# Order of the expert units in a two-layer hybrid decoder trunk: light units in groups of eight, two of them behind the last gate piece, five early loads as single units

## The chip, the cores and the metric

The kernel runs on one core of one Trainium2 chip. The metric is device time in microseconds (us) of one execution; lower is better. The profile is one execution recorded by the hardware profiler.

## The reference

The program is a causal trunk of two layers over 256 tokens with 1024 channels, float32. Each layer adds a mixer (differential attention and retention, gated and projected) and then a feed-forward block: a dense SwiGLU block in layer 0, and in layer 1 a mixture of eight experts of which each token uses two.

```python
def swiglu(x, w1, w3, w2):
    return (jax.nn.silu(x @ w1) * (x @ w3)) @ w2

def moe(hn, w_router, w1, w3, w2):
    ...
    top_v, top_i = lax.top_k(logits, TOP_K)
    top_w = jax.nn.softmax(top_v, axis=-1)
    ...
    for e in range(N_EXPERTS):
        out = out + combine[:, e:e + 1].astype(t.dtype) * swiglu(t, w1[e], w3[e], w2[e])
```

The change touches only the expert block: 1024 to 2816 to 1024, eight times.

## The kernel before

**Units.** Weights come from HBM in units of 128 partitions by 2048 float32, 1 MiB each. An expert has 33 units: 22 hold w1 and w3 (numbers 0 to 21), 11 hold w2 (22 to 32). Eight experts are 264 units, 264 MiB. They are loaded in pairs of two units (2 MiB, one DMA), the last unit of an expert alone. `LOADS` is the list of these 136 loads in the order of issue, all from the SP queue. They go round a ring of six buffers of two units (`RING = 6`), so load i may be issued only when what load i-6 brought is no longer needed.

**Two kinds of unit.** The experts are worked in the order of their token counts; p is the place in it. For p in `CHAIN` (0, 1, 3, 5) up to 128 rows are held, and a weight unit is used in split form: ScalarE copies it to `wh` (L616), VectorE takes the rest to `wl` (L634), and TensorE makes three products for each of four chunks, 12 matmuls (L639 to L641). There are three slots of `wh` and `wl`, and a unit is split two units of this kind ahead (`AHEAD = 2`), so the split of one waits until TensorE has used the one three before it. I call these split units. For p in `SMALL` (2, 4, 6, 7) at most 64 rows are held; TensorE multiplies the loaded unit as it is, in two halves of 64 columns of the array (`few_halves`, L1737). I call these light units, and write 5.30 for unit 30 of place 5.

**When a buffer comes free.** In `load_ring`, a load that follows a split load waits for `lo_ready` of its last unit (both units split), one that follows a light load waits for `unit_used` (TensorE has multiplied both).

**The order.** `moe_orders` walks the split loads and puts two light loads (four units) in front of a split load whenever that many are due. `TAKEN`, unit by unit `IN_USE`, is the order in which all compute engines work; there the light loads stand one split load earlier than in `LOADS`. Both begin and end alike: 0.0 to 0.7, 0.22, 0.23 first, and 5.30, 5.31, 5.32 followed by the light units 7.18 to 7.32 last. Before, TensorE works 31 groups of light units, nearly all of four.

**Gate pieces.** w1 and w3 are worked in slices of 512 columns (the last of 256). After each slice TensorE's result goes through ScalarE (sigmoid, L1147), VectorE (L2413, L2420), four or, for the last, two transposes on TensorE (`g_transposes`, L1263), ScalarE (L1155) and VectorE (L2426), and only then may the units of w2 that use it be multiplied. In `large_unit` of TensorE the transposes of the last piece stand behind unit 30, and units 31 and 32 wait for `g_lo`. The text calls this the last turning; that of place 5 is the last of the program.

**The end.** After 5.32 ScalarE copies the sums to `ys`, GpSimd stores them to HBM and gathers every token's rows back (L844), VectorE adds them (L2441). Beside this TensorE works 7.18 to 7.32 and sums the last expert's rows, which VectorE adds at the very end (L2505), and the result is stored.

Of the kernel before, what the change touches and what calls it, by code (L numbers as in the profile page):

```python
# [52 lines left out]
UNIT = 2048  # L53
RAW, SPLIT = 6, 3
SLICES = FF // 256
IN_GROUPS = IN_W // 512
MIX_UNITS = 2 * IN_GROUPS + 4 + 4
FFN_UNITS = 2 * SLICES + FC // 2
WIDE = FF // 512
# [9 lines left out]
SMALL = (2, 4, 6, 7)  # L69
# [4 lines left out]

CHAIN = tuple(p for p in range(E) if p not in SMALL)
FEW_FROM, FEW_ALONE = 6, 12
RING = 6


def by_slices():  # L80
# [14 lines left out]
def loads_of(p):  # L95

    order = range(FFN_UNITS) if p in SMALL else BY_SLICES
    return [(p, j, min(2, FFN_UNITS - j)) for j in order if j % 2 == 0]


def moe_orders():

    chain = [load for p in CHAIN for load in loads_of(p)]
    few = [load for p in SMALL for load in loads_of(p)]
    n_chain, n_few = (sum(count for _, _, count in loads) for loads in (chain, few))
    loaded, taken, done, n = [], [], 0, 0
    for load in chain:
        loaded.append(load)
        taken.append(load)
        n += load[2]  # L110
        due = max(0, n - FEW_FROM) * (n_few - FEW_ALONE) // (n_chain - FEW_FROM)
        while due - done >= few[0][2] + few[1][2]:
            for _ in range(2):
                loaded.append(few[0])
                taken.insert(len(taken) - 1, few[0])
                done += few.pop(0)[2]
    return loaded + few, taken + few


def units_in(loads):  # L120
    return [(p, j + a) for p, j, count in loads for a in range(count)]


LOADS, TAKEN = moe_orders()
LOADED, IN_USE = units_in(LOADS), units_in(TAKEN)
NUMBER = {unit: MOE_BASE + k for k, unit in enumerate(LOADED)}
USED = {NUMBER[unit]: MOE_BASE + k + 1 for k, unit in enumerate(IN_USE)}
LOAD_OF = {NUMBER[p, j + a]: (i, a) for i, (p, j, count) in enumerate(LOADS) for a in range(count)}


def is_whole(n):

    return MOE_BASE <= n < OVER_BASE and LOADED[n - MOE_BASE][0] in SMALL


def used(n):

    return USED.get(n, n + 1)


SPLITS = [n for n in range(OVER_BASE) if not is_whole(n)]
SPLIT_NO = {n: k for k, n in enumerate(SPLITS)}
# [57 lines left out]
def build(nc, x, boot_d, positions, units_d, pairs_d, lasts_d, zeros_d, cols_d, rows_d, out):  # L200
    ctx = ExitStack()
    with ctx:
# [3 lines left out]
        def sem(name):  # L206
            return ctx.enter_context(nc.semaphore(name))
# [73 lines left out]
        def row(name):  # L281
# [56 lines left out]
        ring = [raw[:, 0:2, :].rearrange("p a n -> p (a n)"), ring_1[:, :], raw[:, 2:4, :].rearrange("p a n -> p (a n)"),  # L338
                raw[:, 4:6, :].rearrange("p a n -> p (a n)"), ring_4[:, :], ring_5[:, :]]
# [10 lines left out]
        landed = [sem(f"landed{s}") for s in range(RAW)]  # L350
        loaded = [sem(f"loaded{s}") for s in range(RING)]
        hi_ready = sem("hi_ready")
        lo_ready = sem("lo_ready")
# [147 lines left out]
        class Units:  # L501
# [40 lines left out]
            def raw(self, j):  # L542

                n = self.number(j)
                if self.in_ring(j):
                    i, half = LOAD_OF[n]
                    return ring[i % RING][:, half * UNIT:(half + 1) * UNIT]
                return raw[:, n % self.raw_slots, :]

            def landed(self, j):  # L550

                n = self.number(j)
                if self.in_ring(j):
                    i, _ = LOAD_OF[n]
                    return loaded[i % RING], 16 * (i // RING + 1)
                s = n % self.raw_slots
                if self.raw_slots == RAW:
                    c = n // RAW + 1
                else:
                    c = len([m for m in range(MOE_BASE) if m % RAW == s])  # L560
                    c += len([m for m in range(OVER_BASE, n + 1) if m % SPLIT == s])
                return landed[s], self.at(16 * c - (16 if s < FIRST else 0), 16 * (self.per // self.raw_slots))
# [10 lines left out]
        def last_in(slots):  # L573

            return max(n for n in range(MOE_BASE) if n % RAW in slots)

        def load_ring(eng, i, e):

            p, j, count = LOADS[i]
            if i >= RING:  # L580
                q, first, n = LOADS[i - RING]
                m = NUMBER[q, first + n - 1]
                eng.wait_ge(*((unit_used, used(m)) if is_whole(m) else (lo_ready, SPLIT_NO[m] + 1)))
            elif i == 1:
                eng.wait_ge(mt_tr, 4 * DEPTH)
            elif i == 4:
                eng.wait_ge(unit_used, MOE_BASE)
            elif i == 5:
                eng.wait_ge(hg_ready, 2)
            else:  # L590
                slots = {0: (0, 1), 2: (2, 3), 3: (4, 5)}[i]
                eng.wait_ge(lo_ready, SPLIT_NO[last_in(slots)] + 1)
            to = ring[i % RING]
            if count == 2:
                eng.dma_start(to, pairs_d[e * (FFN_UNITS // 2) + j // 2]).then_inc(loaded[i % RING], 16)
            else:
                eng.dma_start(to[:, 0:UNIT], lasts_d[e]).then_inc(loaded[i % RING], 16)
# [110 lines left out]
        def _(sp):  # L708
# [28 lines left out]
            for i, (p, _, _) in enumerate(LOADS):  # L737
                if p not in e_of:
                    if len(e_of) == 1:
                        sp.wait_ge(order_ready, 1)  # L740
                    e_of[p] = sp.value_load(otab[0:1, 1 + BY_COUNT[p]:2 + BY_COUNT[p]], min_val=1, max_val=MIDDLE)
                load_ring(sp, i, e_of[p])
# [1933 lines left out]
```

## Time and profile before

| | us |
|---|---|
| median of 3 runs | 1207.55 (1206.71 to 1207.64) |
| the profiled execution, its own time | 1206.29 |
| its span in the profile | 1204.6 |
| TensorE busy | 1189.1 (99%) |
| VectorE busy, ScalarE busy | 741.1 and 593.6 |
| DMA, whole span | 384.82 MB, mean 319 GB/s |

The profiled execution took 1.7 us more than its span, and lies 1.26 us below the median. A busy TensorE in the profile says that matmuls were under way, not that it ran at its peak. The expert block's first load is issued at 509.48 us, its first unit is multiplied at 550.01 us, and the span ends at 1204.6 us.

### The profile page before, as it was taken

What the parts mean: (1) busy time and instruction counts of PE and PEld (TensorE: products, weight loads), DVE (VectorE), ACT (ScalarE), POOL (GpSimd) and SP (SyncE); (2) the same over time, 40 slices, a digit from 0 to 9 for tenths busy, and PEclk for the clock granted to TensorE, in tenths of its full rate; (3) what the DMA queues carried; (4) which work ended last, traced back from release to release, by engine and by line L of the source; (5) the groups of instructions that cost most, each with busy time, mean ns of one, the idle gap of its engine ahead of it and who ended that gap; (6) DMA issues with size and microseconds to landing.
All of it is one profiled execution on the core that took longest, in us unless ns stands there. A gap on an engine that the chain in (4) does not pass through costs nothing.

```text
span 1204.6 us, 15901 instructions
## 1 busy us (share of the span) xinstructions
PE 1189.1 (99%) x6454; PEld 916.8 (76%) x6454; DVE 741.1 (62%) x765; ACT 593.6 (49%) x641; POOL 68.0 (6%) x55
## 2 busy tenths in 40 slices
PE   9999999999999999999999999999999999999997
PEld 8878888888888888888777766777667777577764
DVE  6867765656545857767757565665646665564633
ACT  7667445434336467445554454453535444453420
POOL 0600001000000600000000000000000000000001
PEclk9999999999999999999999999999999999999999
DMA  9753557655555453378999999999999999999997
GB/s 378 310 185 130 177 177 286 217 176 178 205 180 186 159 208 113 111 277 340 384 427 425 427 426 427 427 429 427 426 427 428 427 427 428 426 428 428 427 425 292
DMA packets 36590, 384.82 MB, mean 319 GB/s; under 512 B 4337, under 2 KB 4337, under 8 KB 7985
## 3 DMA queue, kind: packets, MB, share of 16 engines
q1 hardware_dynamic: 34672, 374.83, 77.2%
q0 software_dynamic: 1696, 8.66, 2.0%
q8 instruction: 53, 0.87, 0.3%
q10 hardware_dynamic: 144, 0.26, 0.1%
q14 instruction: 25, 0.20, 0.0%
HBM read 379.80 MB, written 7.61 MB: 322 GB/s over the span
## 4 chain that ended last, share of the span: by engine, by line
PE 86%; DMA 6%; issue 3%; DVE 3%; POOL 1%; ACT 1%; SPq 0%; POOLq 0%; DVEq 0%; ACTq 0%
PE ps L639 21%; PE ps L641 21%; PE ps L640 21%; PE ps L1737 16%; DMA raw<-in_pairs 4%; PE ps L1263 3%; DVE wl L634 1%; DMA h<-in_x 1%; DMA back<-y_rows,yidx 1%; PE ps L1625 1%; POOL rst L777 1%; PE ps L1637 1%; PE ps L1322 1%; ACT wh L616 0%; DVE h L2441 0%
## 5 line engine op out<-in xcount | busy, mean ns | idle before, releaser
L634 DVE TENSOR_TENSOR wl<-raw,wh 128x2048 fp32r<-128x2048 f32 x152 | 350.5, 2309 | 200.0 <-ACT wh L616 199.6
L616 ACT ACTIVATE wh<-raw 128x2048 fp32r<-128x2048 f32 x152 | 291.1, 1918 | 211.1 <-PE ps L641 167.5
L639 PE MATMUL ps<-wh,XT 128*128 128x512 f32 x856 | 340.1, 397 | 0.3 <-DVE wl L634 0.3
L641 PE MATMUL ps<-wh,XT 128*128 128x512 f32 x856 | 333.9, 390 | 0.0
L640 PE MATMUL ps<-wl,XT 128*128 128x512 f32 x856 | 333.4, 389 | 0.0
L634 DVE TENSOR_TENSOR wl<-ring,wh 128x2048 fp32r<-128x2048 f32 x66 | 151.0, 2291 | 89.8 <-ACT wh L616 89.2
L639 PEld LDWEIGHTS ps<-wh,XT 128*128 128x128 f32 x856 | 160.7, 188 | 40.3 <-issue 8.1
L641 PEld LDWEIGHTS ps<-wh,XT 128*128 128x128 f32 x856 | 160.6, 188 | 34.3
L640 PEld LDWEIGHTS ps<-wl,XT 128*128 128x128 f32 x856 | 160.9, 188 | 31.5
L616 ACT ACTIVATE wh<-ring 128x2048 fp32r<-128x2048 f32 x66 | 126.4, 1915 | 95.4 <-PE ps L641 70.1
L1737 PE MATMUL ps<-ring,few_X 128*64 128x256 f32 x704 | 80.6, 381 | 1.5 <-DMA ring<-in_pairs 1.5
L1737 PE MATMUL ps<-raw,few_X 128*64 128x256 f32 x704 | 80.4, 381 | 1.0 <-DMA raw<-in_pairs 1.0
L639 PE MATMUL ps<-wh,moe_gT_h 128*128 128x512 f32 x176 | 70.9, 403 | 2.1 <-DVE moe_gT_l L2426 2.1
L1737 PEld LDWEIGHTS ps<-ring,few_X 128*64 128x64 f32 x704 | 50.4, 137 | 28.1 <-issue 6.5
L1737 PEld LDWEIGHTS ps<-raw,few_X 128*64 128x64 f32 x704 | 49.5, 137 | 28.3 <-issue 5.8
L640 PE MATMUL ps<-wl,moe_gT_h 128*128 128x512 f32 x176 | 69.4, 394 | 0.0
L641 PE MATMUL ps<-wh,moe_gT_l 128*128 128x512 f32 x176 | 69.2, 393 | 0.0
L1737 PE MATMUL ps<-raw,few_gT 128*64 128x256 f32 (+1 forms) x272 | 44.2, 470 | 0.0
L639 PEld LDWEIGHTS ps<-wh,moe_gT_h 128*128 128x128 f32 x176 | 33.4, 190 | 12.9 <-issue 3.9
L942 ACT ACTIVATE mix<-ps,rn 128x512 f32<-128x512 f32 x40 | 26.0, 687 | 27.2 <-PE ps L641 27.1
L641 PEld LDWEIGHTS ps<-wh,moe_gT_l 128*128 128x128 f32 x176 | 33.5, 190 | 7.3
L640 PEld LDWEIGHTS ps<-wl,moe_gT_h 128*128 128x128 f32 x176 | 33.4, 190 | 6.5
(294 smaller groups left out, 1149.1 us busy)
## 6 DMA issues: line engine op xcount, KB each, us to landing
raw<-in_pairs SPq DMA_DIRECT2D x65, 2048.0 KB, 17.6
ring<-in_pairs SPq DMA_DIRECT2D x63, 2048.0 KB, 17.6
raw<-in_units SPq DMA_DIRECT2D x86, 1024.0 KB, 5.0
ring<-in_lasts SPq DMA_DIRECT2D x4, 1024.0 KB, 15.6
raw<-in_lasts SPq DMA_DIRECT2D x4, 1024.0 KB, 17.2
y_rows<-in_zeros POOLq DMA_DIRECT2D x7, 512.0 KB, 7.9
raw<-in_boot SPq DMA_DIRECT2D x5, 512.0 KB, 7.6
y_rows<-ys POOLq DMA_DIRECT2D x4, 512.0 KB, 10.6
```

The costliest lines, as they stand in the source:

```text
L616: nc.scalar.activation(wh[:, U.split_slot(j), :], U.raw(j), ACT.Copy).then_inc(hi_ready, 1)
L634: nc.vector.tensor_tensor(wl[:, s, :], U.raw(j), wh[:, s, :].bitcast(F32), ALU.subtract).then_inc(lo_ready, 1)
L639: nc.tensor.matmul(o, xh, bh, start=start, stop=False)
L640: nc.tensor.matmul(o, xh, bl, start=False, stop=False)
L641: return nc.tensor.matmul(o, xl, bh, start=False, stop=stop)
L777: nc.gpsimd.tensor_tensor(to, of, nhalf[:, 0:of.shape[-1]], ALU.pow).then_inc(rs_ready, 1)
L942: ins = nc.scalar.activation(to, acc, ACT.Copy if g < 6 else ACT.Sigmoid, scale=rn[:, t:t + 1])
L1263: return nc.tensor.transpose(o, i, ident)
L1322: last = nc.tensor.matmul(ps[:, (6, 6, 4)[k] + c, a * n:(a + 1) * n], qkT[part, hd, tok[t]], qkT[part, 4 + hd, 0:n], start=True, stop=True)
L1625: last = nc.tensor.matmul(ps[:, ROWS_AT[n], a * P:(a + 1) * P], xs[:, at:at + P], sel[:, t * SEQ:t * SEQ + P], start=t == 0 and a == 0, st ...
L1637: last = nc.tensor.matmul(ps[:, FEW_ROWS[n], a * P:(a + 1) * P], xs[:, at:at + P], sel[:, t * SEQ + P:(t + 1) * SEQ], start=t == 0 and a == 0,
L1737: last = nc.tensor.matmul(o[at], x, of[half], start=start, stop=stop, tile_position=(0, half * FEW))
```

## The change

`GROUPED = 4`: light loads are taken four at a time, eight units. The order becomes, for example, 0.0 to 0.7, 0.22, 0.23, 0.8 to 0.11 (fourteen split units), 2.0 to 2.7, then eight split units, eight light ones and so on; 17 groups in place of 31. `with_turning_covered` takes the two light units that stand last in front of 5.30 and puts them behind it, in the order of work alone. `SINGLY` is loads 7 to 11: each becomes two DMAs of one unit, and each of those waits only for the split of the unit that lay in its half of the buffer; the counts of landed loads are changed to fit.

```diff
+GROUPED = 4
 RING = 6
+SINGLY = range(RING + 1, 2 * RING)
...
-        while due - done >= few[0][2] + few[1][2]:
-            for _ in range(2):
+        while due - done >= sum(count for _, _, count in few[:GROUPED]):
+            for _ in range(GROUPED):
...
+def with_turning_covered(units):
+
+    first = (CHAIN[-1], 2 * SLICES + 2 * WIDE - 2)
+    few = [unit for unit in units[:units.index(first)] if unit[0] in SMALL][-2:]
+    rest = [unit for unit in units if unit not in few]
+    at = rest.index(first) + 1
+    return rest[:at] + few + rest[at:]
...
-LOADED, IN_USE = units_in(LOADS), units_in(TAKEN)
+LOADED, IN_USE = units_in(LOADS), with_turning_covered(units_in(TAKEN))
...
+            if i in SINGLY:
+                q, first, _ = LOADS[i - RING]
+                for a in range(2):
+                    eng.wait_ge(lo_ready, SPLIT_NO[NUMBER[q, first + a]] + 1)
+                    at = slice(a * UNIT, (a + 1) * UNIT)
+                    eng.dma_start(ring[i % RING][:, at], pairs_d[e * (FFN_UNITS // 2) + j // 2][:, at])\
+                        .then_inc(loaded[i % RING], 16)
+                return
```

How it moves instructions is seen at three places. The first is the SP queue from load 5 on (in the first fence, from the sixth load of the ring; buffers 0, 2 and 3 of the ring print as `raw`). Before:

```order
L595 DMA ring<-in_pairs 128x4096
L741 TENSOR_LOAD otab
L741 ISA x2
L595 ISA
L595 DMA raw<-in_pairs 128x4096
L595 ISA
L595 DMA ring_63<-in_pairs 128x4096
L595 DMA raw<-in_pairs 128x4096 x2
```

The same place with the change:

```order
L619 DMA raw<-in_pairs 128x4096
L601 DMA ring_63<-in_pairs 128x2048 x2
L765 TENSOR_LOAD otab
L765 ISA x2
L601 ISA
L601 DMA raw<-in_pairs 128x2048
```

Load 6 no longer brings a light pair but 0.10 and 0.11, so it stands ahead of the read of the experts' order (`otab`), and load 7 (0.24, 0.25) and those behind it are halves of 2048 columns.

The second place is VectorE from the split of 0.22 to the first pieces of place 2 (`wl` is the split, `moe_gbuf` and `moe_gT_l` belong to the gate pieces of split experts, `few_` to light ones). Before:

```order
L634 TENSOR_TENSOR wl<-ring_64,wh 128x2048 x2
L2420 TENSOR_TENSOR moe_gbuf<-ps,moe_gbuf 128x512
L634 TENSOR_TENSOR wl<-ring,wh 128x2048 x2
L2458 TENSOR_TENSOR few_gbuf<-ps,few_sgm 128x256
L2426 TENSOR_TENSOR moe_gT_l<-ps,moe_gT_h 128x512
L634 TENSOR_TENSOR wl<-raw,wh 128x2048 x2
L2413 TENSOR_TENSOR moe_gbuf<-ps,moe_sgm 128x512
L634 TENSOR_TENSOR wl<-raw,wh 128x2048 x2
```

With the change:

```order
L658 TENSOR_TENSOR wl<-ring_64,wh 128x2048 x2
L2444 TENSOR_TENSOR moe_gbuf<-ps,moe_gbuf 128x512
L658 TENSOR_TENSOR wl<-ring,wh 128x2048 x2
L2450 TENSOR_TENSOR moe_gT_l<-ps,moe_gT_h 128x512
L658 TENSOR_TENSOR wl<-raw,wh 128x2048 x2
L2437 TENSOR_TENSOR moe_gbuf<-ps,moe_sgm 128x512
L658 TENSOR_TENSOR wl<-ring_63,wh 128x2048 x2
L2482 TENSOR_TENSOR few_gbuf<-ps,few_sgm 128x256
```

The splits of 0.10, 0.11, 0.24 and 0.25 now stand ahead of the first light group's work.

The third place is TensorE at the last turning, from the last matmuls of 5.30 to the first of 5.31 (`cols,moe_gbuf` are the turning's transposes, L1761 with the change is L1737 before). Before:

```order
L641 MATMUL ps<-wh,moe_gT_l 128x512
L1263 MATMUL ps<-cols,moe_gbuf 128x128 x2
L639 MATMUL ps<-wh,moe_gT_h 128x512
L640 MATMUL ps<-wl,moe_gT_h 128x512
```

With the change:

```order
L665 MATMUL ps<-wh,moe_gT_l 128x512
L1287 MATMUL ps<-cols,moe_gbuf 128x128 x2
L1761 MATMUL ps<-ring,few_X 64x256 x16
L1287 MATMUL ps<-cols,few_gbuf 128x128 x2
L663 MATMUL ps<-wh,moe_gT_h 128x512
L664 MATMUL ps<-wl,moe_gT_h 128x512
```

Two light units, 7.16 and 7.17, and the two transposes of their expert's piece now stand between the turning and 5.31.

## Rows read from the trace of the kernel before

**Rows 1.** Windows of the core: each engine's busy us, TensorE clock, DMA share, GB/s.

```profile
570.00:575.00 5.00, 5.00 (x26) 4.14 (x24) 4.85 (x4) 4.36 (x4) 0.00 (x0) 1.00 0.47 118
585.00:590.00 5.00, 5.00 (x42) 3.29 (x39) 2.73 (x3) 2.67 (x3) 0.00 (x0) 1.00 0.93 377
600.00:1100.00 500.00, 498.96 (x2888) 356.06 (x2888) 299.39 (x267) 238.72 (x202) 5.09 (x9) 1.00 1.01 427
```

**Rows 2.** Waits: engine, line, what it waited for, us in total, times, longest.

```profile
PE ps L1737 <- DMA ring<-in_pairs: 1.5, 3, 0.6
PE ps L1737 <- DMA raw<-in_pairs: 1.0, 1, 1.0
...
PEld ps L1737 <- issue: 41.1, 136, 1.4
```

**Rows 3.** Timeline of the SP queue, loads 10 to 15 of the ring.

```profile
577.95 5.78 SPq L595 DMA_DIRECT2D ring<-in_pairs  x2
585.68 0.34 SPq L595 DMA_DIRECT2D raw<-in_pairs  x1
589.13 0.34 SPq L595 DMA_DIRECT2D ring<-in_pairs  x1
596.57 5.79 SPq L595 DMA_DIRECT2D raw<-in_pairs  x2
```

**Rows 4.** Windows of one us after a load that starts from rest.

```profile
572.00:573.00 1.00, 1.00 (x6) 0.84 (x5) 1.00 (x2) 1.00 (x1) 0.00 (x0) 1.00 0.71 131
573.00:574.00 1.00, 1.00 (x6) 0.81 (x6) 0.85 (x2) 0.64 (x2) 0.00 (x0) 1.00 0.97 180
574.00:575.00 1.00, 1.00 (x6) 0.84 (x5) 1.00 (x1) 1.00 (x1) 0.00 (x0) 1.00 0.57 229
```

**Rows 5.** Timeline of TensorE around the first light group.

```profile
581.97 3.67 PE L1737 MATMUL ps<-raw,few_X 128*64 128x256 f32 x32
...
589.02 0.50 PE L639 MATMUL ps<-wh,XT 128*128 128x512 f32 x1
```

**Rows 6.** Timeline of ScalarE and VectorE: the split of 0.9.

```profile
578.97 1.92 ACT L616 ACTIVATE wh<-ring 128x2048 fp32r<-128x2048 f32 x1 [0.80 <-PE ps L641]
...
580.92 2.29 DVE L634 TENSOR_TENSOR wl<-ring,wh 128x2048 fp32r<-128x2048 f32 x1 [0.35 <-ACT wh L616]
```

**Rows 7.** Timeline of TensorE from 7.16 to 7.18, the last turning between.

```profile
1145.57 3.67 PE L1737 MATMUL ps<-ring,few_X 128*64 128x256 f32 x32 [0.56 <-DMA ring<-in_pairs]
...
1149.37 0.48 PE L639 MATMUL ps<-wh,XT 128*128 128x512 f32 x1
...
1154.93 0.39 PE L639 MATMUL ps<-wh,moe_gT_h 128*128 128x512 f32 x1
...
1157.71 0.44 PE L1263 MATMUL ps<-cols,moe_gbuf 128*128 128x128 f32 x2
1160.24 0.66 PE L639 MATMUL ps<-wh,moe_gT_h 128*128 128x512 f32 x1 [2.10 <-DVE moe_gT_l L2426]
...
1167.50 4.75 PE L1737 MATMUL ps<-raw,few_X 128*64 128x256 f32 x42
```

**Rows 8.** Timeline of ScalarE and VectorE: splits of 5.30 and 5.31, last piece.

```profile
1150.35 1.92 ACT L616 ACTIVATE wh<-raw 128x2048 fp32r<-128x2048 f32 x1 [8.31 <-DMA raw<-in_pairs]
...
1152.30 4.50 DVE L634 TENSOR_TENSOR wl<-raw,wh 128x2048 fp32r<-128x2048 f32 x2 [6.22 <-ACT wh L616]
...
1157.23 0.42 DVE L2420 TENSOR_TENSOR moe_gbuf<-ps,moe_gbuf 128x256 f32<-128x256 f32 x1
```

**Rows 9.** Window of the core over 5.31, columns as in rows 1.

```profile
1160.00:1164.00 4.00, 3.76 (x10) 2.95 (x11) 0.19 (x1) 0.00 (x0) 0.00 (x0) 0.57 1.01 430
```

**Rows 10.** Chain and timeline at the end: gather back, last sums, last additions.

```profile
1181.51 11.89 DMA back<-y_rows,yidx
...
1195.11 2.00 PE L1823 MATMUL ps<-ys,selT 64*128 64x256 f32 x16
...
1197.58 2.73 DVE L2505 SCALAR_TENSOR_TENSOR h<-ps,comb,h 128x512 f32<-128x512 f32 x4 [0.22 <-DVE h L2441]
```

More of the change, by code:

```diff
@@ L121, in units_in @@
     return [(p, j + a) for p, j, count in loads for a in range(count)]
+def with_turning_covered(units):
[4 more added lines that the diff above has]
+    return rest[:at] + few + rest[at:]
 LOADS, TAKEN = moe_orders()
-LOADED, IN_USE = units_in(LOADS), units_in(TAKEN)
+LOADED, IN_USE = units_in(LOADS), with_turning_covered(units_in(TAKEN))
 NUMBER = {unit: MOE_BASE + k for k, unit in enumerate(LOADED)}
 USED = {NUMBER[unit]: MOE_BASE + k + 1 for k, unit in enumerate(IN_USE)}
+assert all(LOADS[i][2] == LOADS[i - RING][2] == 2 and LOADS[i - RING][0] not in SMALL for i in SINGLY)
 LOAD_OF = {NUMBER[p, j + a]: (i, a) for i, (p, j, count) in enumerate(LOADS) for a in range(count)}
@@ L554, in landed @@
                     i, _ = LOAD_OF[n]
-                    return loaded[i % RING], 16 * (i // RING + 1)
+                    return loaded[i % RING], 16 * len(range(i % RING, i + 1, RING)) + 16 * halved_before(i)
                 s = n % self.raw_slots
@@ L575, in last_in, with halved_before @@
             return max(n for n in range(MOE_BASE) if n % RAW in slots)
+        def halved_before(i):
+            return len([k for k in SINGLY if k <= i and k % RING == i % RING])
         def load_ring(eng, i, e):
             p, j, count = LOADS[i]
+            if i in SINGLY:
[6 more added lines that the diff above has]
+                return
             if i >= RING:
```

## Prediction

> **What bounds the kernel now.** I read the windows first. From 600 to 1100 us the DMA engines are full at 427 GB/s while TensorE is busy 498.96 of 500 us at full clock [rows 1], so either could be the bound. The waits decide: from about 1100 us on TensorE waits for loads, 1.5 and 1.0 us in all [rows 2]. One unit is 1,048,576 bytes, 2.46 us at 427 GB/s. TensorE needs 2.78 us for a split unit (5.56 us for two from 1149.37 to 1154.93 [rows 7]) and 1.76 us for a light one (7.05 us for four [rows 5]); one of each plus its share of transposes is some 4.65 us, against 4.91 us for the two loads. So TensorE starts late, with the ring full, and slowly catches up with a DMA stream that never stops. The end is the place of the stream plus what comes behind it: the pair 5.30, 5.31 lands at 1150.35 [rows 8], 5.32 is multiplied by 1167.5 [rows 7], and from there two chains of nearly equal length run to the end: store and gather back (the gather lands at 1193.4), and fifteen light units with the last sums at 1195.1 to 1197.1. VectorE's last additions start at 1197.58 [rows 10]. Both hang on 5.32, so a delay of 5.32 is a delay of the end, and a gain on one of the chains alone is worth under 0.5 us.
>
> What matters is therefore (1) when the stream becomes full, (2) whether it stays so, (3) the 17.15 us from the landing of 5.30 to the end of 5.32.
>
> **Groups of eight.** The same units are loaded and multiplied; 31 groups become 17. Each switch costs TensorE's queue about 0.3 us (41.1 us in 136 gaps in front of light matmuls [rows 2]), so 14 fewer are at most 4.2 us of TensorE's time. I cost it at nothing: the stream hides it, since TensorE ahead of time only waits longer for loads.
>
> **The stream's start.** Loads 12 and 13 now follow split loads, not light ones. Before, they could be issued at 585.68 and 589.13, when 2.1 and 2.3 were multiplied [rows 3]. Now load 12 waits for the split of 0.11 and load 13 for that of 0.25, and these wait for TensorE's use of 0.8 and 0.10, three split units earlier. 0.8 now starts where the first light unit did, at 581.97 [rows 5], and is used at 584.75; ScalarE's start to VectorE's end is 4.24 us in the split of 0.9 (578.97 to 583.21 [rows 6]); with 0.2 us to start and 0.2 to issue, load 12 goes out at 589.4. Likewise 0.10 is used at 590.2, and load 13 goes out at 594.9.
>
> A load that starts from rest moves 131, 180 and 229 KB in its first three us in place of 427 each [rows 4], a loss of 1.7 us. Before: load 10, issued at 577.95, counts from 579.7 and is through at 584.6; load 11 (the second of the first row, 583.40) follows to 589.5; the window to 590 is short by 0.6 us (377 GB/s [rows 1]); so load 12 moves from 590.1 and load 13 from 595.0. With the change load 11 is through by 588, load 12 starts from rest, counts from 591.1, and load 13 moves from 596.0, 1.0 us later than before. Bounds: 0.3 us later if load 12 loses nothing beyond the 1.0 us until its first packets, 2.0 us if load 13 finds a half-empty queue too. I take **+1.3 us**, nearest to the worked case.
>
> **Single units.** Loads 7 to 11 put their first halves out 2 to 3 us earlier, which fills part of the holes such as 570 to 575 us (118 GB/s [rows 1]). I cost it at nothing, gain or loss: the next load (12) cannot go before 589.4, by which time loads 7 to 11 are through with either form, so what is gained is given back as a longer hole in front of load 12. Nobody waits for them earlier: TensorE's next waits are at 1100 us. The five more issues are 0.33 us each on SP, which otherwise sits in waits. Load 6 no longer waits for the experts' order, but it queues behind load 5 anyway. The Trainium skill, Perfetto Trace Analysis, DMA Optimizations, says that splitting DMAs lets some start sooner where the DMA engines are generally idle; by it the stream would be full earlier, and the sum would lose the 1.3 us and more. That is the first rival below.
>
> **Does the stream stay full?** Load 14 waits for 2.1, now used at about 596.6, and is needed at 601; load 21, at the end of the first eight split units, is free at about 632 and needed at 635. These are the thinnest margins. Sixteen units take TensorE some 37.4 us and the stream 39.3, so the margin grows by 1.9 us a turn. Cost nothing; up to 1 us in the range.
>
> **The last turning.** The loads are the same here, so 5.30 lands at 1150.35 + 1.3 = 1151.65. Before, TensorE was busy with 5.20 and 5.21 until 1154.93 [rows 7], 0.3 us after 5.30's split was ready (1152.30 plus half of 4.50 [rows 8]). Now 7.16 and 7.17 no longer stand in front of them, and TensorE is through early: 7.14 and 7.15 land one pair before 7.16 (1145.5 [rows 7], less 4.9, plus 1.3: 1141.9), take 3.5 us, 5.20 and 5.21 take 5.6, so TensorE stands idle from 1151.1 to 1156.0. Then 5.30 (2.75). The transposes wait 0.3 us for VectorE, which finishes the last piece 0.85 us after the splits (1157.65 against 1156.8 [rows 8], now 1158.95), and take 0.45; 7.16 and 7.17 take 3.5 and their transposes 0.4; the turning's own chain over ScalarE and VectorE is done within that. 5.31 starts 7.5 us after 5.30, before 5.3 (1154.93 to 1160.24, of it 2.1 idle [rows 7]): +2.2 us. 5.31 and 5.32 took 7.26 us, since the clock in the window 1160 to 1164 was 0.57 [rows 9]; without an idle stretch before them they take 5.6: -1.7 us. 5.30's earlier start after landing: -0.3 us. Sum **+0.2 us**: two light units of work, which stood where TensorE had slack, replace an idle stretch and its slow clock, and are worth the same.
>
> **The clock.** An idle stretch of 2.1 us was followed by half clock, 3.4 us long by the loss (7.26 against 5.56 is 1.7 us) [rows 7, 9]. The new idle stretch in front of 5.30 is 4.9 us. If TensorE is at 1.2 GHz when it resumes, 5.30 and what follows lose up to 3 us; nothing if the slow stretch falls into the idle time. The 0.3 us wait for VectorE takes part of it. I take **+1.2 us**, below the 1.7 us of the rows. The Trainium skill, TensorE: Matmul & The Clock Gate, Loop structure matters more than you think, names a DMA wait in front of matmuls as the order that lets the array go cold; by it this change moves the cold stretch from 5.31 to 5.30, and the sum would carry the whole 1.7 us.
>
> **Sum.** 1.3 + 0.2 + 1.2 = +2.7 us on the profiled execution: 1209.0. That execution lies 1.26 us below the median; against the median 1207.55 it is **1210.2 us**.
>
> **Rivals.**
> - The early halves count (faster). If the stream is limited by the holes at 555 to 580 us and load 12's wait is shorter than I work out, the hole of 3.6 us at 570 to 575 (427 less 118 GB/s [rows 1]) comes off: 1204.0. It decides if load 12 is issued before about 586. For: the holes are there. Against: the split of 0.11 needs 0.8 used, and that is TensorE's pace. 8%.
> - TensorE is the bound (faster). Then the 14 switches give up to 4.2 us: 1203.4. For: 498.96 of 500 us busy. Against: the waits for DMA at the end [rows 2] and the full stream. 5%.
> - The stream slips less than 1 us and the slow clock falls into the idle stretch (no difference): 1207.55 + 0.3 to 1.0 + 0.2, 1208.0 to 1208.8. Nothing in the profile excludes it. 39%.
> - The stream is starved in the middle (slower): eight split units in a row free buffers at TensorE's and VectorE's pace, and where load 21's margin of 3 us is gone, each of the first groups leaves a hole of 1 to 3 us: 1211 to 1215. Against: the margins above. 6%.
> - The change does not do what it says: the order shows that it does. Not counted.
>
> **How the numbers follow.** My forecast, slower by 1.5 to 4.5 us, has 42%, most of it past 2.4 us. About 0.2% (2.4 us) is what can be told from no change. Slower by more than that: 40% (34 of my 42, and the starved stream's 6). Within 0.2%: 47% (the 39, and 8 of my case). Faster: 13% (the two rivals). The range reaches from 1206.0, which leaves out the two faster rivals, to 1213.2, which holds the bounds of stream and clock (2.0 + 0.2 + 3.0 is 1212.8) and part of the starved case. Likeliest case's own range: 1209.0 to 1212.0.
>
> **What would show it.** Right: windows from 590 us full at 427 GB/s in both, but load 12 issued at 589 to 590 and load 13 at about 595, a hole around 588 to 590; 5.30 landing 1 to 2 us later, TensorE idle 4 to 5 us in front of 5.30, no idle between the turning's transposes and 5.31, a clock below 1 near 1153 to 1160, 5.32 through at 1169 to 1171. Wrong: windows below 420 GB/s after 600 us, or load 12 before 586, or 5.32 through by 1167.5.

## The result and the profile after

The changed kernel takes **1210.51 us** (median of 9 runs, 1209.66 to 1211.87) against 1207.45 us (9 runs, 1206.16 to 1208.41) for the kernel before on the same chip: ratio 1.0023, 95% interval 1.0015 to 1.0032. It is slower by 3.1 us. The profiled execution has a span of 1207.9 us, before 1204.6. One execution of all those below, of warm_before_last_pair, took 1510.16 us at a mean granted clock of 0.79 and is left out of every median.

**Windows**, columns as in [rows 1].

```profile
570.00:575.00 5.00, 5.00 (x25) 4.15 (x24) 4.85 (x4) 4.64 (x4) 0.00 (x0) 1.00 0.68 223
585.00:590.00 5.00, 5.00 (x24) 4.14 (x23) 4.69 (x4) 3.88 (x4) 0.00 (x0) 1.00 0.65 231
590.00:595.00 5.00, 5.00 (x36) 3.50 (x36) 4.21 (x2) 1.88 (x1) 0.00 (x0) 1.00 0.91 352
600.00:1100.00 500.00, 495.47 (x2873) 358.57 (x2871) 299.97 (x267) 240.26 (x202) 5.11 (x9) 1.00 1.01 427
635.00:640.00 5.00, 5.00 (x50) 3.34 (x48) 0.44 (x2) 0.00 (x0) 0.00 (x0) 1.00 1.01 397
670.00:675.00 5.00, 5.00 (x48) 3.08 (x46) 0.74 (x3) 0.64 (x2) 0.00 (x0) 1.00 1.01 377
```

At 570 us the halves fill part of the hole (223 GB/s for 118 [rows 1]); at 585 the hole is deeper (231 for 377) and reaches into the next window. From 600 to 1100 us the DMA engines are on the whole as full as before (427 GB/s), and TensorE is busy 495.47 us of 500 instead of 498.96: the time it saved became idle time, since the stream sets the pace. Two more dents stand at 635 and 670, with 397 and 377 GB/s where the kernel before has 429 and 439.

**The SP queue** around load 12, at loads 20 and 21, and at the end (us, length of the group of issues).

```profile
575.29 8.05 SPq L601 DMA_DIRECT2D ring<-in_pairs  x4
588.79 0.34 SPq L619 DMA_DIRECT2D raw<-in_pairs  x1
594.23 0.34 SPq L619 DMA_DIRECT2D ring<-in_pairs  x1
...
626.23 7.59 SPq L619 DMA_DIRECT2D raw<-in_pairs  x2
...
1146.58 19.56 SPq L619 DMA_DIRECT2D ring<-in_pairs  x2
```

Load 12 goes out at 588.79 and load 13 at 594.23, where 585.68 and 589.13 stood [rows 3]. Load 21, the second of the fourth row, goes out at 633.49. The last row is the one I had not looked for: load 130 goes out at 1146.58, but load 131, the second of the row, only 19 us later, at 1165.8. Before, load 21 went out at 627.02, and loads 130 and 131 were 4.2 us apart:

```profile
623.04 4.31 SPq L595 DMA_DIRECT2D raw<-in_pairs  x2
...
1145.19 4.56 SPq L595 DMA_DIRECT2D ring<-in_pairs  x2
```

**TensorE at the last turning.** Timeline, with the idle time in front and what ended it.

```profile
1156.79 0.76 PE L663 MATMUL ps<-wh,moe_gT_h 128*128 128x512 f32 x1 [4.73 <-DVE wl L658]
...
1161.94 3.67 PE L1761 MATMUL ps<-ring,few_X 128*64 128x256 f32 x32
...
1171.40 4.97 PE L1761 MATMUL ps<-raw,few_X 128*64 128x256 f32 x44
```

TensorE stands idle 4.73 us in front of 5.30 and not at all in front of 5.31 (2.10 us before [rows 7]). 5.32 is through at 1171.40, 3.9 us later than before. Windows over the same place and behind it:

```profile
1150.00:1155.00 5.00, 2.06 (x10) 1.37 (x8) 0.65 (x1) 2.59 (x2) 0.00 (x0) 0.93 1.00 424
1155.00:1160.00 5.00, 3.21 (x8) 2.56 (x9) 4.90 (x5) 3.19 (x3) 0.00 (x0) 0.50 1.02 436
1160.00:1165.00 5.00, 5.00 (x36) 3.44 (x36) 2.66 (x3) 0.38 (x1) 0.00 (x0) 0.89 0.85 360
1165.00:1170.00 5.00, 5.00 (x27) 3.85 (x24) 0.00 (x0) 0.60 (x1) 0.00 (x0) 1.00 0.83 315
```

The granted clock (third number from the right) is 0.50, the 1.2 GHz level, over 1155 to 1160, and by the three means below 1 for some 6.8 us in all, against 3.4 us before. Some 2.5 of the 6.8 us fall into the idle stretch itself. From 5.30's start to that of the transposes it is 4.84 us (1156.79 to 1161.63), and 2.98 us at full clock (1156.64 to 1159.62 in warm_before_last_pair below), so the slow clock cost TensorE 1.9 us. And the weight stream falls to 360 and 315 GB/s at 1160 to 1170: that is load 131, which came late.

**The end**, as in [rows 10].

```profile
1184.55 9.96 DMA back<-y_rows,yidx
```

```profile
1194.53 2.68 DVE L2465 SCALAR_TENSOR_TENSOR h<-back,tw,h 128x1024 f32<-128x1024 f32 x2 [12.33 <-DMA back<-y_rows,yidx]
...
1198.90 2.00 PE L1847 MATMUL ps<-ys,selT 64*128 64x256 f32 x16
...
1200.02 2.73 DVE L2529 SCALAR_TENSOR_TENSOR h<-ps,comb,h 128x512 f32<-128x512 f32 x4 [0.22 <-DVE h L2465]
```

The gather is four DMAs, issued 1.2 to 1.4 us apart. The row of the changed kernel is the first of them and that of rows 10 the second, so the two can't be set side by side. Before, the first and the additions of the second are

```profile
1180.16 1.05 POOL L844 DMA_INDIRECT back<-y_rows,yidx  x1 [10.74 <-DMA y_rows<-ys]
...
1193.43 1.29 DVE L2441 SCALAR_TENSOR_TENSOR h<-back,tw,h 128x1024 f32<-128x1024 f32 x1 [1.31 <-DMA back<-y_rows,yidx]
```

So the first is issued 4.4 us later than before and is there 9.96 us after its issue, against 10.67 us before (its additions started at 1190.83). The last sums start 3.8 us later, the last additions 2.4 us.

### The profile page after: what moved, and what is told of

Same layout as the page of the kernel before. It is cut to its first block, busy times and chain, and to the rows that moved or that the text cites. A ratio compares the mean times of both kernels' runs of the same rounds, so it can differ in the third digit from the quotient of the medians.

```text
span 1207.9 us, 15914 instructions
## 1 busy us (share of the span) xinstructions
PE 1186.0 (98%) x6454; PEld 919.8 (76%) x6454; DVE 740.6 (61%) x765; ACT 594.2 (49%) x641; POOL 68.0 (6%) x55
## 4 chain that ended last, share of the span: by engine, by line
PE 78%; DMA 13%; DVE 4%; ACT 2%; issue 2%; POOL 1%; SPq 0%; DVEq 0%; POOLq 0%; ACTq 0%
PE ps L663 20%; PE ps L665 20%; PE ps L664 20%; DMA raw<-in_pairs 12%; PE ps L1761 10%; PE ps L1287 3%; DVE wl L658 2%; ACT wh L640 2%; PE ps L1649 1%; DMA back<-y_rows,yidx 1%; POOL rst L801 1%; PE ps L1661 1%; PE ps L1346 1%; PE ps L685 0%; PE ps L689 0%
## 5 line engine op out<-in xcount | busy, mean ns | idle before, releaser
L1761 PE MATMUL ps<-raw,few_X 128*64 128x256 f32 x768 | 87.2, 381 | 3.9 <-DMA raw<-in_pairs 3.9
L1761 PEld LDWEIGHTS ps<-raw,few_X 128*64 128x64 f32 x768 | 56.0, 137 | 32.0 <-issue 8.5
L1761 PE MATMUL ps<-ring,few_X 128*64 128x256 f32 x640 | 73.2, 381 | 1.9 <-DMA ring<-in_pairs 1.9
L1761 PEld LDWEIGHTS ps<-ring,few_X 128*64 128x64 f32 x640 | 46.5, 137 | 24.4 <-issue 4.9
L1189 ACT ACTIVATE few_sgm<-ps 128x256 f32<-128x256 f32 (+1 forms) x24 | 8.7, 361 | 102.7 <-PE ps L1761 102.7
L2482 DVE TENSOR_TENSOR few_gbuf<-ps,few_sgm 128x256 f32<-128x256 f32 (+1 forms) x24 | 9.6, 400 | 67.0 <-ACT few_sgm L1189 58.0
L1761 PE MATMUL ps<-ring,few_gT 128*64 128x256 f32 (+1 forms) x256 | 41.4, 475 | 0.0
```

The lines of the kernel that those rows point to most:

```text
L1761: last = nc.tensor.matmul(o[at], x, of[half], start=start, stop=stop, tile_position=(0, half * FEW))
```

## The experiments

All were timed in five rounds beside the kernel before, whose median was 1207.6 to 1207.7 us (27 to 35 runs); each has 11 runs, first_group_four 4, and the changed kernel the 9 of above. "Shift" is how much later a load's first packet moves than in the kernel before, from the bytes of the packets of the SP queue summed in order. A profiled execution as a whole starts the expert block 0.4 us early to 1.6 us late, so shifts are given less that of load 5, which no edit touches. Read them to 0.1 or 0.2 us. The last column is the profile's own time, without that correction, when the light units behind 5.32 begin (before: 1167.50 [rows 7]).

| kernel | median us | ratio, 95% | shift of load 14 | 30 | 130 | 131 | 5.32 through |
|---|---|---|---|---|---|---|---|
| changed | 1210.51 | 1.0023 (1.0015 to 1.0032) | 1.5 | 2.0 | 2.0 | 3.5 | 1171.40 |
| groups_only | 1209.82 | 1.0017 (1.0008 to 1.0026) | 1.6 | 2.3 | 2.3 | 2.3 | 1169.63 |
| no_singles | 1210.27 | 1.0024 (1.0015 to 1.0033) | 1.6 | 1.7 | 1.6 | 3.2 | 1172.08 |
| no_turning | 1209.61 | 1.0015 (1.0006 to 1.0024) | 1.4 | 2.2 | 2.1 | 2.1 | 1169.74 |
| first_two_fours | 1209.73 | 1.0017 (1.0008 to 1.0026) | -1.9 | 2.3 | 2.3 | 3.1 | 1170.74 |
| singles_only | 1207.78 | 0.9999 (0.9991 to 1.0008) | -2.0 | -0.4 | 0.3 | 0.3 | 1166.33 |
| turning_only | 1208.61 | 1.0007 (0.9998 to 1.0016) | -0.2 | -0.3 | 0.2 | 1.5 | 1169.73 |
| warm_before_last_pair | 1209.68 | 1.0018 (1.0009 to 1.0027) | 1.3 | 1.5 | 1.5 | 2.4 | 1169.43 |
| before_warm_turning | 1207.35 | 0.9998 (0.9989 to 1.0007) | 0.1 | -0.1 | 0.2 | 0.2 | 1166.14 |
| turning_loads_too | 1207.63 | 1.0000 (0.9990 to 1.0009) | -0.1 | -0.3 | -0.1 | -0.1 | 1164.37 |
| change_loads_too | 1209.98 | 1.0021 (1.0012 to 1.0030) | 1.5 | 1.6 | 1.7 | 1.7 | 1166.68 |
| before_late_last_pair | 1208.62 | 1.0006 (0.9997 to 1.0015) | 0.1 | -0.2 | 0.3 | 0.3 | 1170.60 |
| first_group_four | 1223.38 | 1.0136 (1.0121 to 1.0152) | -2.3 | 2.0 | 16.4 | 16.6 | 1164.87 |

### One part, and all but one

```diff
 groups_only:  GROUPED = 4; SINGLY = range(0); IN_USE = units_in(TAKEN)
 no_singles:   SINGLY = range(0)
 no_turning:   IN_USE = units_in(TAKEN)
 singles_only: GROUPED = 2; IN_USE = units_in(TAKEN)
 turning_only: GROUPED = 2; SINGLY = range(0)
```

groups_only: 

> The groups of eight alone, without the covered turning and without single loads. My theory (the groups make loads 12 and 13 wait for splits and shift the stream by 1 to 2 us; the covered turning adds its own 1 to 2 us): about 1209.2 us, 1.7 us over the kernel before; load 12 issued at about 588.8, 5.30 landing 1.6 to 2.1 us later than before, TensorE idle for less than 3 us at the turning. Rival (the groups of eight cost nothing, all of the loss is the covered turning): 1207.5 us and 5.30 landing at 1150.4.

no_singles: 

> The whole change but loads 7 to 11 as pairs. My theory (single loads are worth nothing, since load 12 waits for the split of 0.11 anyway): 1210.5 us, within 0.7 us of the change; load 12 issued at 588.8 and load 13 at 594.2 as with the change, the hole in front of load 12 smaller and the earlier ones larger. Rival A (the singles cost time, as more DMAs): 1209 us. Rival B (they gain time that the groups lose elsewhere): 1212 us or more, 5.30 landing later than with the change.

no_turning: 

> The whole change but the two light units back in front of 5.20. My theory: TensorE has no 4.7 us of idleness in front of 5.30; it stands idle 2.1 us behind the turning as before and loses 1.7 us to half clock there; 5.32 through 17.2 us after 5.30 lands (with the change 19.0), so about 1209.2 us. Rival (the covered turning gains what it was written for, and the loss is all in the stream): 1211 us or more.

singles_only: 

> The kernel before with loads 7 to 11 as single units, nothing else. Theory revised after the run with the first two groups of four (load 12 moved 2.3 us earlier there): the halves fill the early holes, and in the order of before nothing takes that back, since load 12 was queued 4 us ahead of its turn: stream and 5.30's landing 2 us earlier, 1205.7 us. My prediction's theory (what the halves gain is given back in front of load 12): 1207.7 us, 5.30 landing at 1150.4.

turning_only: 

> The kernel before with 7.16 and 7.17 behind 5.30, nothing else. My theory: the stream up to load 130 stays where it was; TensorE idles about 4 us in front of 5.30 in place of 2.1 us behind it, and load 131 goes out only after 7.17; 5.32 through 0 to 2 us later, according to how much of the half clock falls on matmuls: 1207.7 to 1209.5 us, 1208.3 likeliest. Rival (covering pays when the stream is not late): 1206.0 us.

**Groups** cost 2.1 us alone, two thirds of the change. I had expected 1209.2 and it is 1209.82; that they cost nothing (1207.5) is refuted. Load 12 goes out at 589.46, load 13 at 594.90; the stream stands 1.6 us later at load 14 and 2.3 from load 30 on, and the end moves by as much. The step from 1.6 to 2.3 lies at loads 21 to 23 and 28 to 30; in groups_only the first of these is the clearer one (344 GB/s in its window, where the changed kernel has 397 and the one before 429):

```profile
635.00:640.00 5.00, 5.00 (x48) 3.34 (x50) 1.04 (x3) 0.27 (x2) 0.00 (x0) 1.00 0.97 344
```

**Single units** cost and gain nothing: 1207.78 alone, and 1210.27, where I expected 1210.5, against 1210.51 in the change. For them alone I had by then expected 1205.7, and was wrong; my prediction's reading, 1207.7, held. Alone they do what they are meant to up to load 15, and then give it back. Load 12 goes out at 585.85, the stream is 2.0 us ahead at load 14, and at 595 to 605 us it has two windows below what the kernel before moved there (429 and 428 GB/s):

```profile
595.00:600.00 5.00, 5.00 (x23) 4.13 (x22) 4.74 (x4) 4.31 (x3) 0.00 (x0) 1.00 0.95 370
600.00:605.00 5.00, 5.00 (x44) 2.90 (x44) 2.88 (x4) 0.94 (x3) 0.00 (x0) 1.00 0.98 352
```

The SP queue shows why: loads 15 and 16 go out at 602.18 and 604.03, and in the kernel before at 602.02 and 603.87.

```profile
602.18 0.34 SPq L619 DMA_DIRECT2D raw<-in_pairs  x1
604.03 4.31 SPq L619 DMA_DIRECT2D ring<-in_pairs  x2
```

Those buffers come free at the pace of the compute engines, which the single units do not change.

**The covered turning** alone measured +1.0 us (interval -0.2 to +1.9), in the change +0.9 (against no_turning) or +0.45 (no_singles against groups_only). The runs came near what I expected (turning_only 1208.61 for 1208.3, no_turning 1209.61 for 1209.2), and the rivals by which covering gains (1206.0; 1211 or more) are refuted. Each difference is about as small as its uncertainty; all three have the same sign. In all three the shift grows between load 130 and 131, by 1.3 to 1.6 us, and in no kernel without the covered turning does it.

**The clock** was less regular than I had it. The idle stretch of 2.1 us in front of 5.31 was followed by half clock before and in no_turning (0.88 and 0.78 in two windows, 3.4 us), but not in groups_only and singles_only. In all four TensorE waits there for VectorE's part of the turning, not for a load. Windows of groups_only, where 5.31 starts at 1163.97 behind 2.09 us of idle time:

```profile
1160.00:1165.00 5.00, 2.91 (x13) 2.01 (x13) 3.81 (x5) 1.43 (x2) 0.00 (x0) 1.00 0.99 423
1165.00:1170.00 5.00, 5.00 (x25) 3.86 (x25) 0.00 (x0) 0.86 (x2) 0.00 (x0) 1.00 0.99 423
```

The 4.7 us in front of 5.30 were followed by half clock in all three kernels that have them, for 6.8 us in the changed kernel's profile and 3.4 us in those of no_singles and first_two_fours, and so were the 4.05 us of turning_only and 4.71 us in first_group_four (in front of 5.28). Shorter waits for the last loads behaved both ways: 2.51 us in turning_loads_too and in change_loads_too were followed by full clock, 2.50 and 2.88 us in first_group_four by half clock (the two light units behind each took 5.36 us instead of 3.67).

The mean granted clock of every execution is on record too, and says the same over 9 to 11 runs each: 0.9960 in the changed kernel, no_singles and first_two_fours, 0.9966 in turning_only, 0.9968 to 0.9975 in the three kernels without the covered turning (0.9973 before, 85 runs), and 0.9979 to 0.9986 in the five in which products or the order of loads fill the stretch. In the four with the stretch in front of 5.30, a run whose mean clock is 0.001 lower (2.4 us more at the lower level) is 0.5 us longer, give or take 0.3; in the others no such dependence shows (0.0 to 0.1 us). That is a correlation inside kernels, not an experiment.

### Load 12 early, groups of eight later

```diff
-        while due - done >= sum(count for _, _, count in few[:GROUPED]):
-            for _ in range(GROUPED):
+        size = 2 if done < 8 else GROUPED
+        while due - done >= sum(count for _, _, count in few[:size]):
+            for _ in range(size):
```

> The whole change, but the first group of eight light units taken as two groups of four, as in the kernel before; every group from the second on and the end are the same, load for load from load 12 on. My theory: load 12 and 13 are issued at 585.7 and 589.1 again and the 1.1 us that the stream lost there come back, 5.30 lands at about 1151.0, time about 1209.4. Rival (groups of eight starve the stream all along): 1210.5 us as with the change.

The first eight light units are two groups of four, so loads 12 and 13 follow as before the change; from load 12 on the order of loads is the change's. Load 12 in the SP queue, and windows of the core:

```profile
585.75 0.34 SPq L620 DMA_DIRECT2D raw<-in_pairs  x1
```

```profile
630.00:635.00 5.00, 5.00 (x41) 3.09 (x39) 4.28 (x13) 0.26 (x1) 0.00 (x0) 1.00 0.87 344
635.00:640.00 5.00, 5.00 (x47) 3.34 (x48) 1.05 (x3) 0.40 (x2) 0.00 (x0) 1.00 0.98 347
...
670.00:675.00 5.00, 5.00 (x48) 3.08 (x46) 1.54 (x4) 0.64 (x2) 0.00 (x0) 1.00 0.99 359
```

Load 12 is out at 585.75 and the stream 1.9 us ahead at load 14. By load 24 it is 1.4 us behind, by load 30 2.3, as in groups_only. The time is 1209.73, between my 1209.4 and the rival's 1210.5: in the trace of the stream the rival holds, in the time my own figure is the nearer, and why this kernel is 0.8 us below the changed one is open (the difference is about as large as its uncertainty). So the wait of loads 12 and 13, which I had priced, is only the first place where the order of eight shows. Taken away, the next places (loads 21 to 24, 28 to 30) take the full amount: a stream that gets ahead meets a buffer that TensorE has not released.

### The clock in front of the last pair

```diff
             for p, j in IN_USE:
+                if (p, j) == WARM_AT:
+                    for _ in range(18):
+                        nc.tensor.matmul(ps[:, 1, 0:P], ones[:, :], ones[:, :], start=True, stop=True)
```

> The whole change with 18 products of a constant tile, which nobody reads, in front of 5.30, where TensorE stood idle for 4.7 us. My theory (half clock costs 2.2 us of 5.30 in the profile of the change, 4.3 us of matmuls at half speed): no half clock between 1150 and 1200 us, 5.30 takes 2.75 us in place of 4.8, 5.32 through 1.5 to 2 us earlier, 1208.9 us. Rival (the end is set by the last loads, not by 5.32): 1210.4 us, though the clock is full.

> The kernel before with 8 such products in front of 5.31, in the 2.1 us idle stretch of the last turning. My theory: where the half clock came (7.26 us for 5.31 and 5.32 in place of 5.56) it does not come, 5.32 through at about 1165.8; the light units behind then meet the last loads, so the end gains 0.5 to 1 us: 1206.9 us. Rival (the half clock does not follow this gap in most executions): 1207.7 us.

The second is the kernel before with 8 such products in front of 5.31. The products are of constants and nobody reads them, here and in the kernel with 28 of them below. In the changed kernel they fill the idle stretch, and the clock stays at 1.00. Timeline of TensorE:

```profile
1151.76 4.18 PE L1856 MATMUL ps<-ones 128*128 128x128 f32 x36
1156.64 0.47 PE L664 MATMUL ps<-wh,moe_gT_h 128*128 128x512 f32 x1 [0.70 <-DVE wl L659]
...
1169.43 6.91 PE L1762 MATMUL ps<-raw,few_X 128*64 128x256 f32 x62
```

5.32 is through 2.0 us earlier, yet the time falls only from 1210.51 to 1209.68, about the uncertainty, and halfway between my 1208.9 and the rival's 1210.4. In the kernel before, 5.32 is through 1.4 us earlier and nothing is gained at all (1207.35, ratio 0.9998, where I expected 1206.9). What takes it is seen at the end of that kernel, in TensorE's timeline:

```profile
1190.29 5.65 PE L1738 MATMUL ps<-raw,few_gT 128*64 128x256 f32 x48 [1.76 <-DMA raw<-in_pairs]
1195.87 2.00 PE L1824 MATMUL ps<-ys,selT 64*128 64x256 f32 x16
```

TensorE, ahead of time, waits 1.76 us for one of the last loads, a wait that the kernel before does not have, and the last sums start at 1195.87 instead of 1195.11. The gather is issued 2.1 us earlier too, its second DMA at 1179.39 for 1181.51, and that DMA's additions still start at 1193.39, as before (1193.43).

### The order of loads follows the turning

```diff
 LOADS, TAKEN = moe_orders()
+at = LOADS.index((CHAIN[-1], 2 * SLICES + 2 * WIDE - 2, 2))
+LOADS[at - 1], LOADS[at] = LOADS[at], LOADS[at - 1]
```

> Groups of four and pairs as before, the turning covered by 7.16 and 7.17, and now their load stands behind that of 5.30, 5.31 in the order of loads as well, so the ring's order and TensorE's agree. Theory (the covered turning costs its us because load 131 may not overwrite 7.16, 7.17 until they are multiplied behind 5.30, at 1165 in the changed kernel where it had gone out at 1149, and the stream runs dry once more): load 131 now waits for the splits of 5.30, 5.31 and goes out at about 1152, loads 131 to 135 stand within 0.3 us of before, 5.30 lands at 1148 and 5.32 is through by 1166; time 1207.2 to 1207.8, which is before's, since nothing behind 5.32 can pass the last loads. Rival (the idle stretch and slow clock in front of 5.30 are what costs): still an idle stretch of 2 us or more there and half clock behind it, time 1208.2 or more. Second rival (5.32 sets the end by itself): 5.32 earlier by 1.5 or more gives 1206.2 or less.

> The whole change, and the load of 7.16, 7.17 moved behind that of 5.30, 5.31. Theory: the stream's shift of 1.6 us at load 130 is no longer followed by a second one at 131, so what the turning added goes: about 1209.6, the time of the changed kernel without the covered turning, and 5.32 through by 1168. Rival (the clock in front of 5.30 costs what the turning adds): 1210.5, as the changed kernel.

The first has the edit on turning_only, the second on the whole change. The first came as the theory of load 131 had it (1207.2 to 1207.8). The second lies 0.4 us above that theory (1209.6) and 0.5 below its rival (1210.5), and decides nothing. The SP queue and TensorE in turning_loads_too:

```profile
1146.52 7.63 SPq L621 DMA_DIRECT2D ring<-in_pairs  x2
```

```profile
1164.37 7.13 PE L1763 MATMUL ps<-raw,few_X 128*64 128x256 f32 x64
...
1184.26 3.67 PE L1763 MATMUL ps<-ring,few_gT 128*64 128x256 f32 x32 [1.11 <-DMA ring<-in_pairs]
1190.44 5.60 PE L1763 MATMUL ps<-raw,few_gT 128*64 128x256 f32 x48 [2.51 <-DMA raw<-in_pairs]
1195.98 2.00 PE L1849 MATMUL ps<-ys,selT 64*128 64x256 f32 x16
```

Load 131 goes out at 1153.8, the stream does not slip, 5.30 and 5.31 come one load earlier, so that TensorE does not stand idle for them, 5.32 is through at 1164.37, 3.1 us before the kernel before and 5.4 before turning_only, and the time is 1207.63, that of the kernel before. The 3.1 us come back as waits of 1.11 and 2.51 us for the last loads. In the whole change the same edit lets 5.32 be through 4.7 us earlier (6.2 with the late start of that profile), and the time falls by 0.5 us.

### 5.32 late, the stream untouched

```diff
+                if (p, j) == (5, 31):
+                    for _ in range(28):
+                        nc.tensor.matmul(ps[:, 1, 0:P], ones[:, :], ones[:, :], start=True, stop=True)
```

> The kernel before, with 28 products of constants that nobody reads (6.8 us of TensorE) between the last turning's transposes and 5.31. They cover the idle 2.1 us and the slow clock, and push 5.32's end to about 1170.6, 3.1 later than before, while load 131 has long gone out and the weight stream is as before. My prediction's step (a delay of 5.32 is a delay of the end): time up by 2.7 to 3.1, 1210.3 to 1210.7. Rival (the end is set by the last loads and the gather that shares their DMA engines, which don't move): up by 1.5 at most, 1209.1 or less.

TensorE's timeline:

```profile
1158.76 6.42 PE L1832 MATMUL ps<-ones 128*128 128x128 f32 x56
1170.60 5.62 PE L1738 MATMUL ps<-raw,few_X 128*64 128x256 f32 x50
```

5.32 is through at 1170.60, 3.1 us late, and the median is 0.9 us up (interval -0.4 to +1.8). The rival held in the times. The trace lies between the two: the last sums start at 1198.10 (+3.0), the last additions at

```profile
1198.97 2.73 DVE L2509 SCALAR_TENSOR_TENSOR h<-ps,comb,h 128x512 f32<-128x512 f32 x4 [0.92 <-PE ps L1824]
```

that is +1.4 us. Before, the last additions started 2.47 us behind the last sums' start, here 0.87 us behind it and waiting for them: the sums had 1.6 us of slack behind the additions of the gathered rows, and 3.0 less 1.6 us is the 1.4. Those additions themselves are little later, since the second DMA of the gather, issued 2.6 us later (1184.09), lands only 0.7 us later, its additions starting at

```profile
1194.13 1.28 DVE L2445 SCALAR_TENSOR_TENSOR h<-back,tw,h 128x1024 f32<-128x1024 f32 x1 [0.84 <-DMA back<-y_rows,yidx]
```

instead of 1193.43. What I had taken for two chains hanging on 5.32 are three things that meet: the light chain (5.32), the gather and the last weight loads (the stream).

### One smaller group first

```diff
+        size = GROUPED if done else 2
+        while due - done >= sum(count for _, _, count in few[:size]):
+            for _ in range(size):
```

> The change with its first light group of four units in place of eight, so every later split load stands one light pair earlier in the order of loads: load 12 waits for a light unit again, 5.30, 5.31 are load 124 in place of 126, and nineteen light units are left behind 5.32 in place of fifteen. Theory (each group of eight makes the ring wait for split units somewhere, so only the place of the hole moves; the end is the last loads'): load 12 goes out by 586, but the stream at load 40 stands 1 to 2.5 us behind before's; 5.32 is through about 4 us earlier than in the changed kernel and buys nothing; 1208.8 to 1210.2. Rival (only loads 12 and 13 cost, as my prediction had it): the stream stands within 0.5 us of before's and the time is 1207.0 to 1208.2. Second rival (5.32 sets the end): 1206 or less.

1223.38 us, 13 us above the range I expected, so the time decides between none of my cases; only the stream's delay at load 30, 2.0 us, is what the theory had for load 40 (1 to 2.5). I had worked out where loads 12 and 124 fall, and not what the covered turning does to the ring in this order. The SP queue, and windows of the core:

```profile
1129.06 0.33 SPq L620 DMA_DIRECT2D raw<-in_pairs  x1
1159.27 0.33 SPq L620 DMA_DIRECT2D ring<-in_pairs  x1
```

```profile
1140.00:1145.00 5.00, 5.00 (x18) 4.01 (x17) 4.12 (x3) 2.76 (x2) 0.00 (x0) 0.73 1.01 426
1145.00:1150.00 5.00, 5.00 (x25) 4.12 (x25) 3.41 (x3) 3.38 (x4) 0.00 (x0) 1.00 0.69 293
1150.00:1155.00 5.00, 5.00 (x24) 3.98 (x22) 4.84 (x5) 3.99 (x3) 0.00 (x0) 1.00 0.05 20
1155.00:1160.00 5.00, 5.00 (x41) 3.27 (x41) 2.84 (x3) 0.38 (x1) 0.00 (x0) 1.00 0.02 3
1160.00:1165.00 5.00, 5.00 (x24) 3.88 (x24) 0.00 (x0) 0.62 (x2) 0.00 (x0) 1.00 0.97 338
```

Here the two units put behind 5.30 are 7.12 and 7.13, load 121, with six split units and 5.30 between 7.11 and them. Load 127 wants their buffer and waits for 30 us at the head of the SP queue, and the DMA engines move next to nothing for 10 us. The last four windows lack (134 + 407 + 424 + 89) GB/s times 5 us, 12.3 us at 427 GB/s. It is the 19.56 us row of the changed kernel once more, long enough here for the DMA engines to run dry.

## Why the prediction came out as it did

I said 1210.2 us, with 1206.0 to 1213.2 as the range; it is 1210.51 (against 1207.45 for the kernel before, where I had used 1207.55). My likeliest case, slower by 1.5 to 4.5 us, is what happened, but the sum is nearer than its terms.

- **The stream's start: right mechanism, short at the far end.** Load 12 at 589.4 and load 13 at 594.9 were predicted; they are 588.79 and 594.23 (589.46 and 594.90 in groups_only). I took +1.3 us; the shift is 1.5 at load 14 and 2.0 from load 30 on, and groups alone measured +2.1.
- **"Stays full": wrong by a small amount.** I put nothing on it, with a margin of 3 us at load 21 as the thinnest. Load 21 went out at 633.49, not at 632, and the dents at 635 to 640 and 670 to 675 us show that there was no margin: loads 21 to 24 and 28 to 30 are paced by the ring. Windows below 420 GB/s after 600 us were what I had named as a sign of being wrong. first_two_fours shows that these places, not load 12, set how far behind the stream ends. This is the rival "starved in the middle", to which I gave 6%; in size it is 0.5 to 0.7 us, not 1 to 3 each group. What I left out in the margin was the time from an issue to full rate, which I had put into load 12's sum myself (issued at 589.4, counted from 591.1): load 21, issued 1.5 us before the 635 at which I had it needed, still leaves a dent.
- **Single units at nothing: right.** Given back in front of load 12 with the change, at loads 14 to 16 in the order before. The first rival (faster, 8%) fell: load 12 did not go out before 586 in the changed kernel, and where it did (singles_only, first_two_fours) the time did not follow. The Trainium skill, Perfetto Trace Analysis, DMA Optimizations, says that splitting may let some of the transfers start sooner; the trace agrees (223 GB/s for 118 at 570 us), and the time shows none of it.
- **Switches at nothing: right.** TensorE's 500 us from 600 on hold 3.5 us less busy time, and the time is longer. "TensorE is the bound" (5%) fell. That is some 0.25 us a switch. My 0.3 is near it by luck: it came from 136 gaps in TensorE's loading of weights, which are not the switches of 31 groups.
- **The last turning +0.2 and the clock +1.2: together too much, and a term is missing.** The idle stretches came as worked out (4.73 us in front of 5.30, none in front of 5.31). 5.32 is through at 1171.40, just past the 1169 to 1171 that I gave. The slow clock took 1.9 us of TensorE's time for my 1.2, and 5.30 landed 2.1 us later (ScalarE starts on it at 1152.41) for my 1.3. But in the time the turning with its clock is worth 0.5 to 1.0 us, not 1.4, for two reasons. First, the step "a delay of 5.32 is a delay of the end" fails: 3.1 us later cost 0.9 us (before_late_last_pair), and 1.4 and 3.1 us earlier bought nothing (before_warm_turning, turning_loads_too). The two chains behind 5.32 were not within 0.5 us of each other: the last sums had 1.6 us of slack, and the gather landed 0.7 us later for 2.6 us of later issue. Second, I kept "the loads are the same here" for the whole turning. They are in the same order, but what frees their buffers is not: load 131 waits for 7.16 and 7.17, now multiplied at 1161.94. turning_loads_too takes away that wait, and the idle stretch with it, and the turning's cost is gone.
- **The clock's own share** is not isolated. The changed kernel and warm_before_last_pair differ by 0.8 us, with an uncertainty about as large, and the second also frees load 131 two us earlier, so that is an estimate of what the two cost together. The Trainium skill, TensorE: Matmul & The Clock Gate, Loop structure matters more than you think, has a DMA wait in front of matmuls as what lets the array go cold: the trace agrees behind the stretches of 4.05 to 4.73 us in front of 5.30, where a late load holds up the split (four of four), behind the waits of 2.50 and 2.88 us for late loads in first_group_four, and not behind those of 2.51 us in turning_loads_too and change_loads_too. Stretches of 2.1 us that wait for VectorE were followed by half clock in two of four profiles.

So 3.1 us are: some 2.1 from groups of eight through the stream, some 0.5 to 1.0 from the covered turning through load 131 and a late 5.32, none from the single units. How the second part divides between load 131 and the clock is not settled: in turning_loads_too the idle stretch in front of 5.30, the slow clock and the late load all went together. My sum came out 0.3 us from the measured time because a groups term 0.8 us too small and a turning 0.4 to 0.9 us too large cancel: that is luck. That the last loads alone set the floor of the end was shown only in so far as TensorE and the gather wait for them when 5.32 is early; no kernel here moved the stream alone. None of the kernels beats the one before.

## What to carry to other kernels

Where a stream of loads through a ring sets the pace, an order of work is judged by when it frees each buffer, and one late release at the head of a queue holds every load behind it: move two units of work behind a third and look first at which load wants their buffer. If the order of work changes, change the order of loads with it. A gain at the start of such a stream is kept only as far as the next place where the ring is short, so look for the shortest place, not the first one. And before a delay at the end is counted in full, see what waits for the last load when the work in front of it comes early.

## What the runs showed of the chip that I had not expected

- The gather of rows takes longer the earlier it is issued while weights still stream. Its second DMA, from issue to the start of its additions: 10.0 us when issued at 1184.09 (before_late_last_pair), 11.9 at 1181.51 (before), 14.0 at 1179.39 (before_warm_turning), 14.6 at 1178.43 (turning_loads_too). Between the first and the last of these, 5.7 us of issue became 1.1 us of landing. For its first DMA it is less so: 9.3, 10.7, 11.9 and 11.9 us, 5.7 us of issue for 3.0 us of landing. What holds them back no run here isolates; in all four the rate of the DMA engines falls in the same window, 1190 to 1195 us (233 to 276 GB/s).
- The same 2.1 us idle stretch in front of the same matmul was followed by half clock in two profiles and by full clock in two, and waits of 2.50 and 2.51 us for a load once by half clock and twice by full clock, so one profile does not tell what such a stretch costs.
- With the issue blocked for 30 us, what was queued kept the DMA engines at full rate for more than 15 us: the rate fell only at 1145 to 1150, with the last load issued at 1129.06.
